# Chunk 0's expert search moved up between the projections, with 64 of its u rows fetched and dotted there and 36 of its v rows added by VectorE

## The reference

```python
h = x + W_out[concat(RMSNorm(SBAttn(q, k, v)), ConformerConv(c))]   # [q|k|v|c] = RMSNorm(x) W_in
# y = h + PEER(RMSNorm(h)); PEER for a chunk of 128 tokens xc:
qh = (xc @ wq).reshape(-1, 8, 128)
s1, s2 = qh[..., :64] . k1, qh[..., 64:] . k2        # 128 keys each, per head
v1, i1 = top_k(s1, 16); v2, i2 = top_k(s2, 16)
top_s, pos = top_k(v1[..., :, None] + v2[..., None, :], 16)
experts = (i1 * 128 + i2)[pos]; gates = softmax(top_s)
act = gelu(einsum('chkd,cd->chk', u_tab[experts], xc))
y  = einsum('chk,chkd->cd', gates * act, v_tab[experts])
```

## Time and profile before

| | |
|---|---|
| median of three runs | 3063.16 us |
| the profiled execution's own time | 3061.06 us |
| its span | 3059.3 us |
| TensorE busy | 2673.7 us (87%) |
| VectorE busy | 2072.2 us (68%) |
| ScalarE busy | 885.2 us (29%) |
| GpSimd busy | 1978.0 us (65%) |
| DMA | 1121.49 MB, mean 367 GB/s; the 2048 gathers are 1073.87 MB of it |
| TensorE's mean granted clock | 0.991 of full |

### The profile page before, as it was taken

The page is one execution under the profiler, slowest core; times in us unless marked ns, Lnnn a source line. Parts: engine busy times, 40 slices in busy tenths (PEclk is TensorE's granted clock), DMA queues, the critical chain, the costliest instruction groups (busy, mean ns, idle before and its releaser), DMA issues.

```text
span 3059.3 us, 30354 instructions
## 1 busy us (share of the span) xinstructions
PE 2673.7 (87%) x7737; PEld 1199.9 (39%) x7737; DVE 2072.2 (68%) x5227; ACT 885.2 (29%) x2060; POOL 1978.0 (65%) x2061
## 2 busy tenths in 40 slices
PE   8999779878997899889987999799988999777778
PEld 4455334423352344334442445234443445222223
DVE  1175767876778667876787777877787766854443
ACT  2233232123211432135212542146213632111111
POOL 1000177777777777777777777777777777776775
PEclk9999889999999999999999999999999999999999
DMA  6012499999999999999999999999999999999999
GB/s 243 28 39 73 162 402 409 409 409 409 408 402 407 400 409 408 402 406 388 409 409 408 398 407 404 404 404 395 409 409 406 378 399 409 409 410 410 409 409 357
DMA packets 320464, 1121.49 MB, mean 367 GB/s; under 512 B 36465, under 2 KB 44681, under 8 KB 320296
## 3 DMA queue, kind: packets, MB, share of 16 engines
q0 software_dynamic: 294912, 1073.87, 88.5%
q1 hardware_dynamic: 25384, 45.72, 4.2%
HBM read 1111.01 MB, written 8.45 MB: 366 GB/s over the span
## 4 chain that ended last, share of the span: by engine, by line
DMA 31%; issue 18%; PE 18%; POOL 17%; DVE 3%; ACT 1%; POOLq 0%; ACTq 0%; DVEq 0%
DMA ring_u<-in_peer_u,experts 16%; DMA ring_v<-in_peer_v,experts 15%; PE psum L1480 13%; POOL ring_u L1383 9%; POOL ring_v L1383 8%; DVE ring_u L1798 2%; PE psum L1414 1%; PE psum L983 1%; PE psum L1440 1%; PE psum L1430 1%; PE psum L962 0%; DVE log_keep L1723 0%; PE psum L1468 0%; DVE top_v L1092 0%; ACT L1617 0%
## 5 line engine op out<-in xcount | busy, mean ns | idle before, releaser
L1480 PE MATMUL psum<-ring_v,diag 128*128 128x512 f32 x4076 | 1963.7, 606 | 339.8 <-DMA ring_v<-in_peer_v,experts 211.1
L1798 DVE CUSTOM_DVE_ANT_0 ring_u<-ring_u,psum 128x1024 f32<-128x1024 f32 x1024 | 1243.3, 1218 | 664.2 <-DMA ring_u<-in_peer_u,experts 662.4
L1383 POOL DMA_INDIRECT ring_u<-in_peer_u,experts x1024 | 981.0, 958 | 726.2 <-issue 633.7
L1480 PEld LDWEIGHTS psum<-ring_v,diag 128*128 128x128 f32 x4076 | 705.5, 190 | 1332.6 <-issue 974.1
L1383 POOL DMA_INDIRECT ring_v<-in_peer_v,experts x1024 | 988.2, 965 | 342.9 <-issue 279.8
L1626 ACT ACTIVATE diag<-ident,weights 128x128 f32<-128x128 f32 x1019 | 369.0, 393 | 810.7 <-PE psum L1480 622.7
L491 PE MATMUL psum<-w_sb,xnT 128*128 128x512 f32 x560 | 246.9, 599 | 0.0
L1754 DVE SCALAR_TENSOR_TENSOR acc<-conv_in,taps,acc 128x128 f32<-128x128 f32 x720 | 205.1, 347 | 0.0
L983 PEld LDWEIGHTS psum<-actT,w_kept 128*128 128x128 f32 x1024 | 134.3, 192 | 60.7 <-issue 60.7
L491 PEld LDWEIGHTS psum<-w_sb,xnT 128*128 128x128 f32 x560 | 106.2, 192 | 127.7 <-issue 124.3
L983 PE MATMUL psum<-actT,w_kept 128*128 128x128 f32 x1024 | 134.8, 275 | 0.0
(11 more groups left out here) (191 smaller groups left out, 1413.5 us busy)
## 6 DMA issues: line engine op xcount, KB each, us to landing
ring_u<-in_peer_u,experts POOLq DMA_INDIRECT x1024, 12.3
ring_v<-in_peer_v,experts POOLq DMA_INDIRECT x1024, 12.4
w_sb<-in_w_in SPq DMA_DIRECT2D x4, 2048.0 KB, 19.7
x_in<-in_x SPq DMA_DIRECT2D x8, 512.0 KB, 4.4
w_kept<-in_w_out SPq DMA_DIRECT2D x1, 4096.0 KB, 13.3
h_res<-in_x SPq DMA_DIRECT2D x8, 512.0 KB, 7.0
w_kept<-in_peer_wq SPq DMA_DIRECT2D x1, 4096.0 KB, 14.5
wo_sb<-in_w_out SPq DMA_DIRECT2D x1, 4096.0 KB, 12.8
```

What stands on the lines that cost most here:

```text
L1383: nc.gpsimd.indirect_dma_start(ring[kind][:, at, :], None, peer_u[0] if kind == "u" else peer_v[0], bass.IndirectOffsetOnAxis(S.experts[c ...
L1480: last = nc.tensor.matmul(y_ps[:, j * BANK:(j + 1) * BANK], diag[:, e % DIAGS, :], ring["v"][:, n % RING["v"], j * BANK:(j + 1) * BANK], s ...
L1798: nc.vector.tensor_tensor_reduce(out=row, in0=row, in1=hn, scale=1.0, scalar=0.0, op0=ALU.mult, op1=ALU.add, accum_out=dots[:, e:e + 1]).t ...
```

## The change

- The front of chunk 0 starts with chunk 1's projections and no longer with chunk 4's: scores after Q of chunk 1, `mix` after Q of chunk 3, the query after A of chunk 3, the last scores after G of chunk 3. Its searches run on VectorE beside chunks 3 and 4. Its scratch (`Scratch`) lies in the last two chunks' part of `vals` and in the place of the tap rows. The overlap of chunks 6 and 7 (their projections interleaved) is gone; chunks run one after the other.
- GpSimd gathers u rows 0 to 69 of chunk 0 in the first part, into six of `w_kept`'s eight rows, and VectorE takes dots 0 to 63 beside chunks 5 to 7 (`dot_early`).
- For all chunks the u ring is then those six rows of `w_kept`, and the v ring has 7 slots (six of its own and `w_kept`'s last). `w_kept`'s seventh row is the sum `y_side`. peer_wq is therefore loaded a second time, to `wq_sb`, after the second copy of w_out.
- In chunk 0's 128 slots of the second part a u row is dotted in every second slot (64 are left, 58 of them to be gathered), and 108 v rows are spread over slots 4 to 127 (`first_at`). Every third of them, 36, is added by VectorE into `y_side`, which is added to TensorE's sum in chunk 1's slot 20 (`end_first_y`).

```diff
-RING = {"u": 6, "v": 8}
+RING = {"u": 6, "v": 7}
+EARLY = 4 * TOPK
...
             store_q(LAST)
+            store_h(LAST)
             sp.wait_ge(projected[V], CHUNKS)
             sp.dma_start(wo_sb[:, :, :], w_out[0].rearrange("(k p) n -> p k n", p=P)).then_inc(S.wo_loaded, 16)
-            store_h(LAST)
+            sp.dma_start(wq_sb[:, :, :], peer_wq[0].rearrange("(k p) n -> p k n", p=P)).then_inc(S.wq_loaded, 16)
...
+            pool.wait_ge(S.experts_done, 1)
+            for e in range(EARLY + RING["u"]):
+                if e >= RING["u"]:
+                    pool.wait_ge(S.dotted, e - RING["u"] + 1)
+                at = e % RING["u"]
+                nc.gpsimd.indirect_dma_start(
+                    w_kept[:, at, :], None, peer_u[0],
+                    bass.IndirectOffsetOnAxis(S.experts[0][:, e:e + 1], 0)).then_inc(S.row_in["u"][at], 16)
...
-            first_scores()
-            chunk(CHUNKS - 4, {G: first_transpose_weights})
-            chunk(CHUNKS - 3, {Q: first_attend, K: first_transpose_conv, A: first_transpose_o, G: first_transpose_conv_back})
+            chunk(1, {Q: first_scores, G: first_transpose_weights})
+            chunk(2, {Q: first_attend, K: first_transpose_o, G: first_transpose_conv, V: first_transpose_conv_back})
+            project(3, Q)
             mix_first()
+            project(3, K)
             transpose_h(0)
+            project(3, A)
             query_first()
+            project(3, G)
             score_first()
+            transpose_qk(3)
+            project(3, V)
+            transpose_x(4)
+            transpose_glu(3)
+            for i in range(4, CHUNKS):
+                chunk(i)
...
+            hn_go_live()
+            for i, (lo, hi) in zip(range(5, CHUNKS), ((0, 21), (21, 42), (42, EARLY))):
+                dot_early(lo, lo + 9)
+                norm_qk(i)
+                scale_qk(i)
+                dot_early(lo + 9, lo + 16)
+                glu_(i)
+                dot_early(lo + 16, lo + 18)
+                if i < LAST:
+                    norm_x(i + 1)
+                dot_early(lo + 18, hi)
...
+    first_at = {4 + e * (SLOTS - 5) // CAUGHT: e for e in range(CAUGHT)}
+    SIDE = ([row_of(FIRST, e) for e in range(CAUGHT) if e % 3 == 2]
+            + [row_of(TAIL, e) for e in range(ROWS - LAG, ROWS) if e % 4 == 3])
...
+            def end_first_y():
+                dve.wait_ge(S.taken, FIRST + 2)
+                dve.wait_ge(side_added, FIRST_SIDES)
+                for j in range(2):
+                    at = slice(j * BANK, (j + 1) * BANK)
+                    if j == 0:
+                        dve.wait_ge(half_added, FIRST + 1)
+                    else:
+                        dve.wait_ge(row_added, pe_rows(ROWS - 1))
+                    nc.vector.tensor_tensor(y_out[:, at], y_ps[:, at], y_side[:, at], ALU.add)
```

More of the change, by code:

```diff
@@ L145, in build @@
     gate_sum = keep.tile("gate_sum", [P, 2, PH], F32)
+    experts = [keep.tile(f"experts{n}", [P, ROWS], I32) for n in range(2)]
+    gates = [keep.tile(f"gates{n}", [P, ROWS], F32) for n in range(2)]
+    dots = keep.tile("dots", [P, ROWS], F32)
     late = Map(nc, keep.at)
@@ L150, in build @@
     relu_z = [late.tile(f"relu_z{n}", [P, SEQ], F32) for n in range(2)]
-    experts = [late.tile(f"experts{n}", [P, ROWS], I32) for n in range(2)]
-    gates = [late.tile(f"gates{n}", [P, ROWS], F32) for n in range(2)]
     top_v = late.tile("top_v", [P, PH, 2, TOPK], F32)
@@ L156, in build @@
     best_i = late.tile("best_i", [P, PH, TOPK], U32)
-    assert late.at - keep.at <= 2 * KT_D * BANK * 4
     wo_sb = late.tile("wo_sb", [P, KT_D, D], F32)
+    wq_sb = late.tile("wq_sb", [P, KT_D, D], F32)
     g_mix = vec[:, 0:KT_D]
@@ L558, in first_transpose_conv_back @@
                 last.then_inc(S.cT_ready, 1)
-            mix, transpose_h, query, score_keys = tensor_front(nc, pe, S, (z_ps, z_ps), w_kept, w_kept)
+            mix, transpose_h, query, score_keys = tensor_front(nc, pe, S, W, (z_ps, z_ps), w_kept, w_kept)
             def mix_first():
@@ L743, in chunk @@
                 copy_v(i)
-                copy_xT(i + 1)
+                for piece in after_v:
+                    piece()
+                if i < LAST:
+                    copy_xT(i + 1)
                 copy_glu(i)
@@ L883, in _, with hn_go_live, dot_early @@
             (add_residual, mean_h, norm_h, search_keys, add_candidates, search_candidates, shift_gates,
-             split_positions, look_up, number_experts, _) = vector_front(nc, dve, S, (z_ps, z_ps))
-            def search_first():
-                for part in range(2):
-                    for stage in range(5):
-                        search_keys(0, 2 * stage + part)
-            def chunk(i, after_scale=()):
-                norm_qk(i)
-                scale_qk(i)
-                for piece in after_scale:
-                    piece()
-                glu_(i)
-                norm_x(i + 1)
+             split_positions, look_up, number_experts, _) = vector_front(nc, dve, S, W, (z_ps, z_ps), None)
+            def hn_go_live():
+                dve.wait_ge(S.h_normed, 1)
+                nc.vector.tensor_copy(hn, S.hn_next[:, :]).then_inc(S.taken, 1)
+            def dot_early(lo, hi):
+                for e in range(lo, hi):
+                    if e == 0:
+                        dve.wait_ge(S.taken, 1)
+                    dve.wait_ge(S.row_in["u"][e % RING["u"]], 16 * (e // RING["u"] + 1))
+                    row = w_kept[:, e % RING["u"], :]
+                    nc.vector.tensor_tensor_reduce(out=row, in0=row, in1=hn, scale=1.0, scalar=0.0,
+                                                   op0=ALU.mult, op1=ALU.add,
+                                                   accum_out=S.dots[:, e:e + 1]).then_inc(S.dotted, 1)
             norm_x(0)
@@ L1261, in phase1 @@
     m = Map(nc, base)
-    ring = {kind: m.tile(f"ring_{kind}", [P, RING[kind], D], F32) for kind in "uv"}
+    ring_v = m.tile("ring_v", [P, RING["v"] - 1, D], F32)
+    slots = {"u": [w_kept[:, n, :] for n in range(RING["u"])],
+             "v": [ring_v[:, n, :] for n in range(RING["v"] - 1)] + [w_kept[:, KT_D - 1, :]]}
     diag = m.tile("diag", [P, DIAGS, P], F32)
@@ L1266, in phase1 @@
     ln_stat = small.tile("ln_stat", [P, 8], F32)
-    dots = small.tile("dots", [P, ROWS], F32)
+    dots = S.dots
     geld = small.tile("geld", [P, ROWS], F32)
@@ L1395, in _ @@
         def _(pe):
-            mix, transpose_h, query, score_keys = tensor_front(nc, pe, S, (z_ps, w_ps), wo_sb, w_kept)
+            mix, transpose_h, query, score_keys = tensor_front(nc, pe, S, W, (z_ps, w_ps), wo_sb, wq_sb)
             def scores(f, a, u):
@@ L1480, in add_row @@
                     last = nc.tensor.matmul(y_ps[:, j * BANK:(j + 1) * BANK], diag[:, e % DIAGS, :],
-                                            ring["v"][:, n % RING["v"], j * BANK:(j + 1) * BANK], start=e == 0,
+                                            slot("v", n)[:, j * BANK:(j + 1) * BANK], start=e == 0,
                                             stop=is_last)
@@ L1796, in dot_row @@
                 dve.wait_ge(*landed("u", n))
-                row = ring["u"][:, n % RING["u"], :]
+                row = slot("u", n)
                 nc.vector.tensor_tensor_reduce(out=row, in0=row, in1=hn,
@@ L1888, in step @@
             def step(c, f):
-                if c is not None:
+                if c is not None and later(c):
                     hn_go_live(c)
@@ L1905, in _ @@
             weigh_rows(CHUNKS - 1, PH - 1)
-            for n, e in enumerate(SIDE):
-                add_row_aside(n, e)
+            for n in range(FIRST_SIDES, len(SIDE)):
+                add_row_aside(n)
             end_y()
```

401 lines of the change are left out of this document (210 added, 191 removed).

## The result

The changed kernel takes 2968.36 us, the median of four runs (2962.76 to 2970.55), beside 3063.1 for the kernel before: a ratio of 0.9689 (95% interval 0.9672 to 0.9706), 95 us or 3.1% less. The profiled execution is the fastest of the four, 2962.76 us, and its span is 2961.0.

What follows compares the result with a forecast made beforehand. The DMA's gathers were taken to bound the kernel: 403 until they resume + 2522.9 for 1971 gathers + 72.6 + 12 + 5 = 3015.5 us of span, forecast 3019 us; eight in ten 2987 to 3055, low end 2989, high end 3072.

Steps and rivals of the forecast that it cites:

- The price of a gather: Each 0.524 MB gather costs the DMA 1.28 us, at 409.6 GB/s.
- 1971 x 1.28 (2522.9): Gathers left once GpSimd resumes after the seam, times 1.28 us each: 2522.9 us of the span.
- The first part: Before the seam: `experts` ready and early gathers from 241, TensorE's products ending at 354, 2 us later than before.
- The seam: Between the two parts: q waits behind 8.39 MB of loads until 387, gathers resume at 403, DMA idle about 16 us.
- Now some 26: At the seam: TensorE's first product waits some 26 us for q, against 8.63 before.
- the seam costs nothing: Rival at the seam: q passes the loads in time and first row sums keep ahead: 2989 us, chance 0.18.
- Chunk 0's slots: Second part: 166 gathers in 128 slots, 212.5 us of DMA, with 12 us lost to an uneven front, bounds 0 and 30.
- GpSimd bound in chunk 0: Rival: VectorE's adds hold gathers up; at 1.28 us each, chunk 0 is 28 us longer: 3047 us, chance 0.07.
- about 225 us: Sign to look for: how long chunk 0's slots take in the second part.
- A v ring of 7: Second part: one v slot less costs 5 us, bounds 0 and 27.
- The rival that it starves: Rival, chunks 1 to 7: late TensorE holds v slots, stopping GpSimd: 3068 us, chance 0.08; milder form, no change, 0.05.
- The other fixed terms: Other transfers, thin slices, tail and start, carried over from the kernel before: 72.6 us.

Runs made afterwards that it cites:

- e1: The kernel before with both rings moved to start at a multiple of 512 bytes: 3000.76 us, ratio 0.9801 to the kernel before.
- e9: The kernel before with both rings 256 bytes past a multiple of 512: 3000.17 us, where the kernel before took 3062.58.
- e16: The kernel before with both rings 128 bytes past a multiple of 512: 3060.64 us, where the kernel before took 3061.91.
- e2: The changed kernel with w_kept, so the u ring, moved 64 bytes up: 3019.89 us, ratio 0.9866 to the kernel before.
- e10: The changed kernel with its v ring also 512-byte aligned and the second peer_wq load issued behind chunk 1's q: 2949.12 us, ratio 0.9631 to the kernel before.
- e4: The kernel before with a v ring of 7 slots for 8: 3062.83 us, ratio 1.0002 to the kernel before.

## Why the prediction was wrong

- **The price of a gather** is the step that failed: "1971 x 1.28 (2522.9)". I took 1.28 us for a constant of the chip from a plateau of 409 GB/s, and the changed kernel does it in 1.25. The cause is the start address of the ring, shown by e1, e9 and e16 on the kernel before, and by e2 on the changed one. The change moved one ring to a good address as a by-product of putting it into `w_kept`. e2 is the changed kernel at the old price, and it took 3019.89 us for the 3019 forecast. Of the 95 us gained, then, 43 are the part that I had costed (3063 to 3020) and 52 the address (3020 to 2968). No row of before could show the price at another address, but the code told that the rings' addresses changed, and both ends of the range kept 1.28. No rival had a cheaper gather.
- **The first part** held: 241 forecast for the first early gather, 240.28 measured; 354 and 352.2 for the products' end.
- **The seam** held, in mechanism (small load behind two large ones on one queue) and in size: q at 387 and 390.2, gathers from 403 and 407. e10 shows it from the other side. "Now some 26" for TensorE's wait did not fit the forecast's own times: it stands beside the 8.63 of before, which is counted from the end of the products, and 387 - 354 is 33; the trace has 38.00. The sum used 403 and not the 26. The rival "the seam costs nothing" fell.
- **Chunk 0's slots**: 12 us forecast. From the gather at 407.01 on, the 159 that were left of the 166 took 215.3 us, until this one of the changed kernel:

```profile
622.27 0.94 POOL L1451 DMA_INDIRECT w_kept<-in_peer_u,experts  x1 [0.31 <-issue]
```

  At 1.25 us each they would take 198.8, so 16.5 us were lost, 11.7 of them from 510 to 630 (120 x (1 - 378/419)). In e2, at the old price, the same stretch took 217.2 us, 13.6 over 159 x 1.28. The size was about right and the reason half wrong. I had it from VectorE's sum of work; from 510 to 630 GpSimd was the bound, because the adds lengthen its issues. I had this as the rival "GpSimd bound in chunk 0", at 0.21 us per add and 8 us in all, or with chance 0.07 at 1.28 per add and 28 us. From 407 to 650 the truth lay between: 64 issues beside 35 adds, 0.24 us longer each, 15 us in all. The "about 225 us" for the slots also counted the seven gathers issued before 403; the sum did not.
- **A v ring of 7**: 5 us forecast. In the kernel before, e4 measured 1 us with an interval of -2 to +4; the changed kernel was not tried with eight slots. The rival that it starves is out: behind chunk 0 (slices 10 to 39) the changed kernel's slices lie under its plateau by 28 us in all, those of the kernel before by 29.
- **The other fixed terms** (72.6 us) stood: of the rest of 90.2 us, 16.5 are chunk 0's and about 1 the v ring's, which leaves 72.7. That 90.2 meets the forecast's 89.6 so closely is luck, as chunk 0 cost 4 us more and the ring 4 less.

## What to carry to other kernels

Before a DMA's rate is taken for a constant, look at where each of its buffers starts: here 256-byte alignment of the rings was worth 2% of the kernel, more than the reordering itself, and one line in the kernel before gets it. When a transfer gets cheaper, ask for the next floor at once; here it was GpSimd's issue of 1.24 us, 0.04 us below. And ask of every small load that something waits for what stands ahead of it in its queue: 13 us came back for moving one line.
